# The last merge's gate tiles computed inside the fifth branch's four groups

## The reference, cut to what matters

```python
proj = h @ P['w_in']
u_a, qkv_b, z_b, a_b, b_b, x_c, gate_c, z_d, xbc_d, dt_d, gate_raw = _split(proj, IN_SPLITS)
# S5 branch (k = 0): per group of 16 channels a complex diagonal recurrence, then GLU
xs_re, xs_im = associative_scan(lambda_bar * x + B u)
y = C_re xs_re - C_im xs_im + D * u;  y = gelu(y);  y = y * sigmoid(y @ s5_w_glu)
# merge, k over the four branches
merged = sum_k sigmoid(gate_raw[k]) * (branch_k @ w_branch[k])
x = x + g_m * (merged @ w_out)
```

## Time and profile before

| | |
|---|---|
| median of 3 runs | 3329.8 us |
| profiled execution | 3327.37 us |
| its span | 3325.3 us |
| mean granted clock of PE | 0.932 |
| store of one gate unit (192 KB), median to landing | 1.8 us |

### The profile page before, as it was taken

The page is one execution under the profiler, slowest core; times in us unless marked ns, Lnnn a source line. Parts: engine busy times, 40 slices in busy tenths (PEclk is TensorE's granted clock), DMA queues, the critical chain, the costliest instruction groups (busy, mean ns, idle before and its releaser), DMA issues. The chain is left out here.

```text
span 3325.3 us, 27376 instructions
## 1 busy us (share of the span) xinstructions
PE 2891.7 (87%) x10827; PEld 1736.9 (52%) x10827; DVE 1120.1 (34%) x1718; ACT 662.8 (20%) x1120; POOL 48.8 (1%) x56
## 2 busy tenths in 40 slices
PE   6998999978999996993999456998959999999963
PEld 3556777754555663551555444554534444444431
DVE  4794344433131554314016491112340000000024
ACT  2442222213011112004000752000210010100101
POOL 0000000000000000000000000000000000000010
PEclk9999999979999998996999778999969999999976
DMA  6001111121001013001001001002055655473122
GB/s 253 26 26 61 59 69 57 38 98 69 26 26 51 27 50 143 26 26 50 4 22 51 26 0 51 26 0 108 19 221 190 272 202 191 184 270 151 45 96 100
DMA packets 37516, 283.28 MB, mean 85 GB/s; under 512 B 4113, under 2 KB 13713, under 8 KB 26385
## 3 DMA queue, kind: packets, MB, share of 16 engines
q1 hardware_dynamic: 30048, 254.80, 19.7%
q0 software_dynamic: 7344, 26.74, 2.4%
HBM read 340.80 MB, written 41.39 MB: 115 GB/s over the span
## 5 line engine op out<-in xcount | busy, mean ns | idle before, releaser
L474 PE MATMUL psum<-arena 128*128 128x384 f32 x3552 | 1166.6, 492 | 88.0 <-DVEq L302 59.0
L474 PEld LDWEIGHTS psum<-arena 128*128 128x128 f32 x3552 | 681.9, 192 | 570.3 <-DVEq L302 62.1
L1240 PE MATMUL psum<-arena 128*128 x1056 | 461.6, 595 | 1.9 <-ACT arena L1576 1.9
L1240 PEld LDWEIGHTS psum<-arena 128*128 128x128 f32 x1056 | 199.1, 191 | 241.0 <-issue 241.0
L634 PE MATMUL psum<-arena 128*128 128x384 f32 x768 | 271.8, 492 | 0.0
L1226 PE MATMUL psum<-arena 128*128 x528 | 232.2, 592 | 1.1 <-DVE arena L2164 1.1
L615 DVE TENSOR_TENSOR arena<-arena,psum 128x1152 f32<-128x1152 f32 x32 | 43.3, 1355 | 447.9 <-PE psum L474 447.9
L634 PEld LDWEIGHTS psum<-arena 128*128 128x128 f32 x768 | 139.1, 192 | 71.2 <-issue 1.8
L2160 DVE TENSOR_TENSOR arena<-arena,psum 128x512 f32<-128x512 f32 x33 | 22.7, 688 | 437.6 <-issue 401.1
L1226 PEld LDWEIGHTS psum<-arena 128*128 128x128 f32 x528 | 97.8, 190 | 112.3 <-issue 112.3
L1125 PE MATMUL psum<-arena 128*128 128x384 f32 x384 | 128.5, 494 | 13.0 <-DMA arena<-in_out 13.0
(11 more groups left out here) (482 smaller groups left out, 2668.0 us busy)
## 6 DMA issues: line engine op xcount, KB each, us to landing
arena<-in_moe SPq DMA_DIRECT2D x33, 4096.0 KB
arena<-in_moe SPq DMA_DIRECT2D x33, 2048.0 KB
arena<-in_ada SPq DMA_DIRECT2D x12, 2048.0 KB, 9.2
y_rows<-arena SPq DMA_DIRECT2D x33, 512.0 KB, 2.6
arena<-in_gate SPq DMA_DIRECT2D x8, 2048.0 KB, 7.9
gate_raw<-arena SPq DMA_DIRECT2D x48, 192.0 KB, 1.8
arena<-gate_raw SPq DMA_DIRECT2D x4, 2304.0 KB, 11.5
arena<-in_br SPq DMA_DIRECT2D x4, 2048.0 KB, 9.7
```

What stands on the lines that cost most here:

```text
L474: last = nc.tensor.matmul(pset(s)[:, n, :], w[:, kk, :], src[:, kk, n * N3:(n + 1) * N3], start=(kk == 0), stop=(kk == K - 1))
L1240: last = nc.tensor.matmul(bank(w), x[:, k * P:(k + 1) * P], arena[:, bass.ds(at + (4096 * w + 512 * k), 512)], start=(k == 0), stop=(k == ...
```

## The change

EARLY_GATES gets gate 0. Its 192 calls are placed in the S5 groups by a third table, `s5_fill_points`: 16, 9, 9, 9 calls after the transposes of groups 0 to 3 (tag "uc"); 27, 32, 32, 34 after the kernel products ("scan"); and 1, 2, 2, 3 after each of the first three output products ("y0" to "y2"). ACT copies finished units after its weight copies, after the copies to `sDD`, and after a product's gelus. The units use banks 6 and 7, so the output products move to banks 0 and 1, and kernel products wait for all gelus of the group before. The staging buffers lie in the end of `Y`, which DVE writes after a new wait. Both halves of gate 0 are loaded to one slot, the one that ua leaves; the second waits for unit 12 of PE. glu goes to the slot of s5_bc, after the group-3 input products. The first half of the raw gates is read back when the last output product is done, the second after phase 11 (it lies where u was).

```diff
-EARLY_GATES = [1, 3]
+EARLY_GATES = [1, 3, 0]
@@ plan_loads
-    def add(*names):
+    def add(*names, same=False):
         for a, g in names:
-            loads.append((a, g, (len(loads)) % 2))
+            loads.append((a, g, 0 if not loads else loads[-1][2] if same else 1 - loads[-1][2]))
...
-    add(("ua", 0), ("s5_bc", 0), ("glu", 0))
+    add(("ua", 0), ("s5_bc", 0), ("gate0", 0))
+    add(("gate0", 1), same=True)
+    add(("glu", 0))
     merge(0)
...
+def s5_fill_points():
+    points, n = [], 0
+    for i in range(4):
+        counts = [("uc", 9 if i else 16), ("scan", (27, 32, 32, 34)[i])] + [("y%d" % q, (1, 2, 2, 3)[i]) for q in range(3)]
+        for tag, k in counts:
+            n = min(n + k, 24 * KD)
+            points.append((i, tag, n))
+    points[-1] = (3, points[-1][1], 24 * KD)
+    return points
+S5_FILL = s5_fill_points()
+S5_COUNT = {(i, tag): n for i, tag, n in S5_FILL}
...
-        mg_tmp3 = cut(Rb, T)
+        mg_early = {1: cut(Rb, T), 3: cut(Rb, T), 0: cut(R0 + 4 * T, T)}
         graw = {...
+                0: [cut(at, 4 * T).rearrange("p (k t) -> p k t", k=4) for at in (31808, R0)]}
@@ sync: the list of loads
+                if (a, g) == ("gate0", 1):
+                    done = 0
+                    for i, tag, n in S5_FILL:
+                        sp_gate_units(sp, 0, done // KD, n // KD)
+                        if done < 12 * KD <= n:
+                            sp.wait_ge(g_fill, 3 * KD * EARLY_GATES.index(0) + 12)
+                            sp.dma_start(W[s], A[a][g]).then_inc(s_w[s], 16)
+                        if (i, tag) == (3, "uc"):
+                            sp.wait_ge(a_ca, 4)
+                            sp.wait_ge(a_v, 4)
+                            sp.dma_start(W[1 - s], A["glu"][0]).then_inc(s_w[1 - s], 16)
+                        done = n
+                    sp.wait_ge(a_y, 16)
+                    sp_gates_back(sp, 0, 0)
+                    before[s] = (a, g)
+                    before[1 - s] = ("glu", 0)
+                    continue
+                if a == "glu":
+                    continue
...
+                if a == "br0":
+                    sp.wait_ge(s_phase, 3 * 11)
+                    sp_gates_back(sp, 0, 1)
@@ tensor: S5
                 last.then_inc(a_wt, 1)
+                fill(i, "uc")
                 pe.wait_ge(a_wc, i + 1)
...
                 if i:
-                    pe.wait_ge(a_dd, i)
+                    pe.wait_ge(a_g, 4 * i)
...
                 last.then_inc(a_k, 1)
+                fill(i, "scan")
...
-                        dst = bank(6 + j % 2)[:, NQ * h:NQ * (h + 1)]
+                        dst = bank(j % 2)[:, NQ * h:NQ * (h + 1)]
...
                     last.then_inc(a_y, 1)
+                    if q < 3:
+                        fill(i, "y%d" % q)
@@ scalar: S5
+            def evict(i, tag):
+                nonlocal done
+                n = S5_COUNT[(i, tag)] // KD
+                act_gate_units(act, 0, done, n)
+                done = n
...
                 nc.scalar.activation(wb[:, 1024:2048], psum[:, 2048:3072], ACT.Copy).then_inc(a_wc, 1)
+                evict(i, "uc")
                 if i < 3:
                     act_chunks(i + 1)
...
                 last.then_inc(a_dd, 1)
+                evict(i, "scan")
...
                     last.then_inc(a_g, 1)
+                    if q < 3:
+                        evict(i, "y%d" % q)
...
-            act_merge(act, 0)
+            act_gates(act, 0)
@@ vector: before the GLU products
+            for i in range(2):
+                dve.wait_ge(g_st[i], 16 * 12 * len(EARLY_GATES))
```

More of the change, by code:

```diff
@@ L333, in build @@
         adaL = cut(21504, 512)
-        stage = {1: [cut(45056 + N3 * i, N3) for i in range(2)], 3: [cut(35840 + N3 * i, N3) for i in range(2)]}
+        stage = {1: [cut(45056 + N3 * i, N3) for i in range(2)], 3: [cut(35840 + N3 * i, N3) for i in range(2)],
+                 0: [cut(20864 + N3 * i, N3) for i in range(2)]}
         condp = cut(45824, 256)
@@ L421, in build @@
         mg_tmp = cut(R0 + 2 * T, T)
-        mg_tmp3 = cut(Rb, T)
+        mg_early = {1: cut(Rb, T), 3: cut(Rb, T), 0: cut(R0 + 4 * T, T)}
         graw = {1: [cut(R0 + (4 + 4 * i) * T, 4 * T).rearrange("p (k t) -> p k t", k=4) for i in range(2)],
-                3: [cut(R0 + (4 - 4 * i) * T, 4 * T).rearrange("p (k t) -> p k t", k=4) for i in range(2)]}
+                3: [cut(R0 + (4 - 4 * i) * T, 4 * T).rearrange("p (k t) -> p k t", k=4) for i in range(2)],
+                0: [cut(at, 4 * T).rearrange("p (k t) -> p k t", k=4) for at in (31808, R0)]}
         gate_raw = {k: nc.dram_tensor("gate_raw%d" % k, (P, KD * T), F32, kind="Internal").ap().rearrange("p (k t) -> p k t", k=KD)
@@ L608, in dve_merge @@
                     V.eng.wait_ge(g_sg, KD * EARLY_GATES.index(k) + m + 1)
-                    sig, tmp = graw[k][m // 4][:, m % 4, :], mg_tmp3
+                    sig, tmp = graw[k][m // 4][:, m % 4, :], mg_early[k]
                 else:
@@ L742, in _ @@
                         sp.wait_ge(s_pstate, 64)
-                    elif pa in ("gate1", "gate3"):
+                    elif pa in ("gate1", "gate3", "gate0"):
                         sp.wait_ge(g_fill, 3 * KD * EARLY_GATES.index(int(pa[4:])) + 12 * (pg + 1))
@@ L746, in _ @@
                         sp.wait_ge(s_phase, 3 * 9)
-                    elif pa == "s5_bc":
-                        sp.wait_ge(s_phase, 3 * 11)
                     else:
@@ L1062, in _, with fill @@
             pe.wait_ge(a_u, 4)
+            units, count = pe_gate_units(pe, 0), 0
+            def fill(i, tag):
+                nonlocal count
+                for _ in range(S5_COUNT[(i, tag)] - count):
+                    next(units)
+                count = S5_COUNT[(i, tag)]
             wb = bc[:, 2048:4096]
@@ L1488, in _ @@
                         last = nc.scalar.activation(u[32 * q:32 * q + 32, k:Q5:4, :],
-                                                    hd(bank(6 + j % 2)[32 * k:32 * k + 32, 0:2 * NQ], 2),
+                                                    hd(bank(j % 2)[32 * k:32 * k + 32, 0:2 * NQ], 2),
                                                     ACT.Gelu_apprx_tanh)
                     last.then_inc(a_g, 1)
+                    if q < 3:
+                        evict(i, "y%d" % q)
             act.wait_ge(a_fin, 4)
```

## The result

The changed kernel took 3230.78 us (median of 4 runs, 3228.10 to 3237.18) beside 3330.93 us for the kernel before on the same chip: ratio 0.9701, 95% interval 0.9688 to 0.9713. That is 100.2 us less; 100.6 was forecast, and 3228. The profiled execution took 3229.76 us at a span of 3227.6.

A forecast was written before the change was run, and what follows sets the result against it. PE is busy 87% of the span, but ACT and DVE end the fifth branch's cycles. Merge -134.9, output weights -4.4 and branch +38.7 give -100.6 us: 3228 us forecast, range 3209 to 3246.

The forecast's parts named there:

- What bounds: Fifth branch before the change: ACT and DVE set the end of a 44.15 us cycle; PE has some 22 us slack.
- The merge: Last merge: 192 gate calls leave, 192 branch matmuls stay, branch weights load beneath the GLU tiles; 134.9 us less.
- Output weights: Before the output projection: first half loads during the branch tiles, only the second is late; 4.4 us less.
- Group 0: Fifth branch, up to group 0's first output product: gate-weight load wait, 16 calls and low clock delay ACT's chunk copies; +4.9 us.
- Group 1: Fifth branch, cycle before of 43.92 us: PE's calls and a wait for ACT lengthen it to 49.9; +6.0 us.
- ACT's hold: Group 1: PE's ninth unit waits until ACT evicts the seventh's bank; 2.5 us.
- Group 2: Fifth branch, cycle before of 44.15 us: 9.6 us wait for second-half gate weights, then low clock; 61.35 long, +17.2 us.
- Group 3: Fifth branch, cycle before of 39.10 us: PE's calls lengthen it to 50.5, ACT never late; +11.4 us.
- The clock: Fifth branch: granted clock left at full except behind two load waits, going by the fourth branch's rows.
- rival 3: Four groups: clock stays at 1.2 instead of 2.4 GHz, calls cost +124, net +24, 3351 us, slower; 3%.
- Rival 1: Fifth branch: ACT and DVE still set cycles, PE's additions cost only the two load waits; -124, 3203 us; 10%.
- rival 2: Fifth branch: in-order PE puts every portion on the chain, 138.7 us against 139.3 won; 3327 us, no change; 3%.

The follow-up runs named there:

- the eviction experiment: Changed kernel with ACT copying one more gate unit in group 1, behind the chunk copies instead of the kernel copies: 3225.57 us, ratio 0.9684.

## Why the prediction was right

- *What bounds*: PE idle behind an ACT and DVE chain, and a merge full of PE. Halving the matmuls and moving calls show that after the change the sum of PE's work and of its three waits sets the groups.
- *The merge*: -134.9 forecast, -134.8 measured; 192 branch matmuls 62.19 us (62.1), the wait 2.73 (2.7). The experiment with late branch weights shows that their load is hidden beneath the GLU tiles. The gates read back, allowed 11 or 12 us, landed after 7.8 (median of two), and none of them held up PE.
- *Output weights*: -4.4 forecast, -4.8 measured. The second half, loaded alone, landed after 8.0 us (7.8 forecast); the wait is back when the first half is held.
- *Group 0*: +4.9, measured 5.0: 4.69 us for the load (4.6) and 12.79 us for 16 calls, 2.4 more than at full clock.
- *Group 1*: the one term off beyond 1 us, +7.6 for +6.0. ACT's hold was right (2.42 for 2.5), but I charged no clock for it, having granted the fall only to two load waits. The windows above show 0.58 behind it; the eviction experiment gives 4.4 us for both.
- *Group 2*: +17.2, measured 16.2. PE waits 9.62 us (9.6); it resumes with 2.2 us of low clock, and the pieces around are a little shorter than summed.
- *Group 3*: +11.4, measured 10.6, at clock 1.00 and no idle time.
- *The clock*: 0.92 to 1.00 in the groups (0.67 to 0.81 before), so rival 3, that low clock through the groups would cost 124 us, did not happen. The Trainium skill ("TensorE: Matmul & The Clock Gate", section "A second HAM failure mode: psum-queue depth-cycling") reports a kernel that cycled through PSUM banks, idled briefly between groups of matmuls and had its clock swing for that. The trace does not show that here: PE goes from one kind of work to the next without gaps, and in the groups the clock falls only behind the waits of 4.69, 2.42 and 9.62 us.
- *Rival 1* (the fill hides, 3203) fails for cycles of 50 and 60 us, *rival 2* (fully exposed, no change) for a growth of 38 us where 138.7 was its price. The argument against rival 1 had one count wrong: 46 to 52 calls are those placed in a group, while a cycle has 44, 47 and 49 of them, as the prediction's own walk through the groups has it, 28 to 32 us. It decides nothing.

Errors of +1.6, -1.0, -0.8 and -0.4 us cancelled, and a sum of the parts right to 0.5 us is luck on top of sound terms. So is the 100.2 us between the medians: the four runs of the changed kernel lie 9 us apart, and its profiled execution is only 97.7 us shorter than the one before.

## What to carry to other kernels

When matmuls are moved into idle time, walk through one cycle with all engines side by side, portion by portion: here 124 us of fill in 94 us of holes lengthened the branch by 38 us, not 30 and not 124, because PE's own work became what sets the cycles, and three waits came with it. Then look for waits that the interleaving itself makes, a second load to a busy slot, an engine that works in order and so evicts late; here one changed line of the table gave back 14 us. And a wait for the second of two loads should stand at the first instruction that reads it.

## What was not expected of the hardware

PE's clock falls while PE is busy throughout. In the last chunk of the GDN branch, where matmuls of 16 columns follow one another, the kernel before shows (windows as above)
```profile
660.00:680.00 20.00, 18.69 (x128) 16.51 (x127) 3.73 (x8) 4.82 (x14) 0.00 (x0) 0.90 0.03 11
680.00:700.00 20.00, 20.00 (x99) 18.64 (x100) 0.94 (x2) 0.60 (x1) 0.00 (x0) 0.59 0.00 1
```
and the kernel after, with the same instructions,
```profile
660.00:680.00 20.00, 18.68 (x118) 16.51 (x117) 3.73 (x8) 4.47 (x13) 0.00 (x0) 0.85 0.03 11
680.00:700.00 20.00, 20.00 (x88) 18.58 (x87) 0.69 (x1) 0.60 (x1) 0.00 (x0) 0.50 0.00 0
```
A group of 16 such matmuls takes 1.86 us at one level and 3.43 at the other, and where the clock falls differs from execution to execution. PE's last hole ahead of the first fall is one of 0.8 us, ending at 672.03 us before and 671.67 after. In the kernel before, the clock rises again at 686 and falls again near 690, and PE is busy all the time from 672 to 700 us; so the second fall has no wait just ahead of it.

The fifth branch's transposes start at 1835.85 to 1840.69 us in the nine profiles of changed kernels, and at 1835.72 in the kernel before. Nearly all of this comes from the GDN chunk: in all ten profiles 1130.3 to 1130.7 us lie between the first matmul of 512 columns behind it (705.31 to 710.11 us) and those transposes. This spread of up to 5 us blurs the totals of the small experiments, whose single cycles can be read much closer (the same to 0.01 us in the two profiles of the changed kernel); whether it is all of the spread of the totals is not shown. No experiment was made on it.

Also: a wait of 2.42 us was followed by a clock of 0.58 in group 1, while waits of 2.73 and 2.87 us ahead of the merge and of the GLU tiles were followed by no fall (192 matmuls in 62.19 us, 96 in 31.20). What differs between them stays open.
